# Cross attention: probability transposes and value products taken for two heads at a time

## The chip, the cores and the metric

One core of one Trainium2 chip. The metric is the device time of one execution in microseconds (us), median of repeated runs. All work is fp32: a product is made of three passes of the matrix engine over operands split into a high and a low half (fp32r); transposes and a few small products run in plain fp32.

## The reference, cut to what matters

Two layers, each with two feed-forward blocks, a mixer and a cross attention. The change touches only the cross attention (4 heads of 256 columns, 256 tokens, 256 memory tokens):

```python
hq = (rms_norm(x, xa_norm[l]) @ xa_wq[l]).reshape(b, t, XA_HEADS, XA_HD)
...
s = jnp.einsum("bqhd,bmhd->bhqm", hq, mk).astype(jnp.float32) * (XA_HD ** -0.5)
p = jax.nn.softmax(s, axis=-1).astype(mv.dtype)
o = jnp.einsum("bhqm,bmhd->bqhd", p, mv).reshape(b, t, XA_HEADS * XA_HD)
x = x + o @ xa_wo[l]
```

## The kernel before

Each engine has its own instruction list, written out by hand in the order in which it runs, and the lists meet at semaphores. `xa_pe`, `xa_act` and `xa_dve` each count the events of one engine in the order listed in the code, and `at(l, event)` is the count to wait for. In the cross attention of a layer:

- PE (TensorE) makes the queries of a head with `queries(l, h)` (48 products), its scores with `S(h)` (12 products), transposes its probabilities with `pT(h)` (four fp32 transposes of 128x128), multiplies by the values with `pv(h)` (12 products) and runs the output projection with `o(h)` (48 products, in two halves `n`, of eight column blocks `d` each; `between` is work put ahead of the second half, `midway` ahead of the fifth column block of that half). `last_down` is the projection of head 3. The weight blocks are q4 and q5 (queries of heads 2 and 3) and o0 to o3.
- DVE (VectorE) scales the queries (`hq_scaled`), takes their low half (`hq_lo_part`), finds the row maximum (`row_max`), divides the exponentials by their sum (`normalise`, whose event `p{h}` lets `pT(h)` run), takes the low half of the transposed probabilities (`pT_lo`, whose event lets `pv(h)` run) and of the head's output (`oT_lo`, whose event lets `o(h)` run), and takes the low half of each weight block (`split`).
- ACT (ScalarE) takes the high halves (`hq_hi_part`, `pT_hi`, `oT_hi`, `split`) and the exponentials (`exp`).

`e_sb` and the halves `p_hi`, `p_lo` hold two heads, so heads 0 and 1 go ahead of heads 2 and 3. The PSUM banks are shared: `pT(0)` to `pT(3)` write banks G[2], G[3], G[0], G[1], and scores and value products of head h use G[h].

The weight blocks stream through a ring of three places of 2048 columns. SP loads a block when DVE has split the one that it overwrites, and ACT splits a block (`split_block`) only when PE has multiplied the block whose place it takes:

```python
if BEFORE[i]:
    act.wait_ge(s_blk, BEFORE[i])
```

With the block widths here o1 takes the place of q4, o2 that of q5, and o3 that of o0. So ACT's split of o3 waits until PE has finished `o(0)`. The first two blocks of the second feed-forward block take the place of o1.

Of the kernel before, what the change touches and what calls it, by code (L numbers as in the profile page):

```python
# [20 lines left out]
KD = D // P  # L21
# [177 lines left out]
def hymba_kernel(nc, x_d, mem_d, memT_d, w_d, par_d, const_d, fin_d, out_d):  # L199
    ctx = ExitStack()  # L200
    with ctx:
# [12 lines left out]
        def signals(name, events):  # L214
            return Signals(sem(name), events)
# [166 lines left out]
                                      "sso1 kvlo5 on1 oT0 oT1").split())  # L382
        att_pool = signals("att_pool", ["bias", "ro0", "ro1"])
        xa_pe = signals("xa_pe", "q0 S0 S1 pT0 pT1 pv0 S2 pv1 S3 pT2 pT3 pv2 pv3".split())
        xa_act = signals("xa_act", "hq0 hq1 exp0 exp1 hq2 pT0 hq3 pT1 oT0 oT1 exp2 exp3 pT2 pT3 oT2 oT3".split())
        xa_dve = signals("xa_dve", "hf0 hf1 hq0 hq1 max0 p0 max1 p1 hf2 pT0 hf3 hq2 hq3 pT1 oT0 max2 oT1 p2 max3 p3 pT2 pT3 oT2 oT3".split())

        SCALE = DK ** -0.5
        XSCALE = XD ** -0.5
# [275 lines left out]
        def _(act):  # L665
# [331 lines left out]
            def cross(l):  # L997
                norm_start(4 * l + 2)
                split(l, "q", 4)
                spread_root(4 * l + 2)  # L1000
                A(junk[:, 0:8], eps[:, :], ACT.Exp)
                split(l, "q", 5)

                def hq_hi_part(h):

                    act.wait_ge(xa_dve.sem, xa_dve.at(l, f"hf{h}"))
                    A(hq_hi[:, 2 * h:2 * h + 2, :], HQ_F[h][:, :, :], ACT.Copy).then_inc(xa_act.sem, xa_act.one(f"hq{h}"))

                def exp(h):

                    act.wait_ge(xa_dve.sem, xa_dve.at(l, f"max{h}"))
                    for t in range(TT):
                        last = A(e_sb[:, h % 2, t, :], s_sb[:, t, 0:T], ACT.Exp, bias=nmx[:, 0, 2 * (h % 2) + t:2 * (h % 2) + t + 1],
                                 accum_out=den[:, 2 * (h % 2) + t:2 * (h % 2) + t + 1])
                    last.then_inc(xa_act.sem, xa_act.one(f"exp{h}"))

                def pT_hi(h):

                    act.wait_ge(xa_pe.sem, xa_pe.at(l, f"pT{h}"))
                    A(p_hi[:, 2 * (h % 2):2 * (h % 2) + 2, :], pair(XA_PT[h]), ACT.Copy  # L1020
                      ).then_inc(xa_act.sem, xa_act.one(f"pT{h}"))

                def oT_hi(h):

                    act.wait_ge(xa_pe.sem, xa_pe.at(l, f"pv{h}"))
                    A(a_hi[:, 2 * h:2 * h + 2, :], pair(XA_O[h]), ACT.Copy).then_inc(xa_act.sem, xa_act.one(f"oT{h}"))

                hq_hi_part(0)
                hq_hi_part(1)
                split(l, "o", 0)  # L1030
                exp(0)
                split(l, "o", 1)
                exp(1)
                hq_hi_part(2)
                pT_hi(0)
                hq_hi_part(3)
                pT_hi(1)
                oT_hi(0)
                split(l, "o", 2)
                oT_hi(1)  # L1040
                exp(2)
                exp(3)
                pT_hi(2)
                split(l, "o", 3)
                pT_hi(3)
                oT_hi(2)
                oT_hi(3)
                for i in heads(l, "ffn2"):
                    split_block(i)
# [40 lines left out]
        def _(dve):  # L1090
# [446 lines left out]
            def cross(l):  # L1537
# [60 lines left out]
                    dve.wait_ge(s_mrbc, 1)  # L1598
                row_max(0)
                split(l, "o", 0)  # L1600
                normalise(0)
                row_max(1)
                split(l, "o", 1)
                normalise(1)
                hq_scaled(2)
                pT_lo(0)
                hq_scaled(3)
                hq_lo_part(2)
                hq_lo_part(3)
                pT_lo(1)  # L1610
                oT_lo(0)
                row_max(2)
                oT_lo(1)
                split(l, "o", 2)
                normalise(2)
                row_max(3)
                normalise(3)
                pT_lo(2)
                split(l, "o", 3)
                pT_lo(3)  # L1620
                oT_lo(2)
                oT_lo(3)
                split_block(heads(l, "ffn2")[0])
# [54 lines left out]
        def _(pe):  # L1678
# [135 lines left out]
                        spread_mean_squares(q)  # L1814
                    four_columns(INDEX[l, "in", i], (U, GATE), range(2 * i, 2 * i + 2), ready=8 * q)

            def head_columns(hi, lo, whi, wlo, bank, ks, width, at=0, ready=None, between=None):

                for k in ks:
                    if k == KD // 2 + 1 and between is not None:  # L1820
                        between()
                    if ready is not None:
                        pe.wait_ge(s_alo, ready + k + 1)
                    for d in range(2):
                        out = bank[:, d * T:(d + 1) * T]
                        w = slice((k - ks[0]) * width + at + d * P, (k - ks[0]) * width + at + (d + 1) * P)
                        M(out, whi[:, w], hi[:, k, :], start=(k, d) == (0, 0), stop=False, skip_group_check=True)  # L1827
                        M(out, whi[:, w], lo[:, k, :], start=False, stop=False, skip_group_check=True)  # L1828
                        last = M(out, wlo[:, w], hi[:, k, :], start=False, stop=k == KD - 1, skip_group_check=True)  # L1829
                return last  # L1830
# [28 lines left out]
                            last.then_inc(xa_pe.sem, xa_pe.one("q0"))  # L1859
                    last.then_inc(s_blk, 1)  # L1860

            def queries(l, h, between):

                whi, wlo = weights(INDEX[l, "q", 2 + h])
                head_columns(a_hi, a_lo, whi, wlo, HQ[h], range(KD), T, between=between).then_inc(s_blk, 1)

            def gate_up_blocks(l, f, c):

# [353 lines left out]
            def cross(l):  # L2222
                pe.wait_ge(att_dve.sem, att_dve.at(l, "kvlo5"))
                first_queries(l, 4 * l + 2)

                def S(h):

                    pe.wait_ge(xa_dve.sem, xa_dve.at(l, f"hq{h}"))
                    for t in range(TT):
                        out = XA_S[h][:, t * T:(t + 1) * T]  # L2230
                        for k in range(2 * h, 2 * h + 2):
                            M(out, hq_hi[:, k, tok(t)], kx_hi[:, k, :], start=(t, k) == (0, 2 * h), stop=False)
                            M(out, hq_hi[:, k, tok(t)], kx_lo[:, k, :], start=False, stop=False)
                            last = M(out, hq_lo[:, k, tok(t)], kx_hi[:, k, :], start=False, stop=(t, k) == (1, 2 * h + 1))
                    last.then_inc(xa_pe.sem, xa_pe.one(f"S{h}"))

                def pT(h, tiles=range(TT)):

                    pe.wait_ge(xa_dve.sem, xa_dve.at(l, f"p{h}"))
                    if h >= 2:  # L2240
                        pe.wait_ge(xa_dve.sem, xa_dve.at(l, f"oT{h - 2}"))
                    for t in tiles:
                        for k in range(2):
                            last = TR(XA_PT[h][:, k * T + t * P:k * T + (t + 1) * P],
                                      e_sb[:, h % 2, t, k * P:(k + 1) * P], ident)
                    if tiles[-1] == TT - 1:
                        last.then_inc(xa_pe.sem, xa_pe.one(f"pT{h}"))

                def pv(h):

                    pe.wait_ge(xa_dve.sem, xa_dve.at(l, f"pT{h}"))
                    for d in range(2):
                        out = XA_O[h][:, d * T:(d + 1) * T]
                        w = slice((2 * h + d) * P, (2 * h + d + 1) * P)
                        for k in range(2):
                            p = 2 * (h % 2) + k
                            M(out, vx_hi[:, k, w], p_hi[:, p, :], start=(d, k) == (0, 0), stop=False)
                            M(out, vx_hi[:, k, w], p_lo[:, p, :], start=False, stop=False)
                            last = M(out, vx_lo[:, k, w], p_hi[:, p, :], start=False, stop=(d, k) == (1, 1))
                    last.then_inc(xa_pe.sem, xa_pe.one(f"pv{h}"))  # L2260

                def o(h, between=None, midway=None):

                    pe.wait_ge(xa_dve.sem, xa_dve.at(l, f"oT{h}"))
                    down(l, "o", h, a_hi, a_lo, (2 * h, 2 * h + 1), h == 0, between=between, midway=midway)

                queries(l, 2, between=lambda: S(0))
                S(1)
                queries(l, 3, between=lambda: pT(0))
                pT(1)  # L2270
                pv(0)
                S(2)
                pv(1)
                o(0, between=lambda: S(3), midway=lambda: pT(2, range(1)))
                pT(2, range(1, 2))
                o(1, between=lambda: (pT(3), pv(2)))
                pv(3)
                o(2)
                pe.wait_ge(xa_dve.sem, xa_dve.at(l, "oT3"))
                last_down(4 * l + 2, a_hi, a_lo, (6, 7))  # L2280
# [110 lines left out]
```

## Time and profile before

| | |
|---|---|
| median of 3 runs | 1123.31 us (1123.18 to 1124.47) |
| the profiled execution | 1123.65 us, of which the span of the instructions is 1121.9 us |
| mean granted TensorE clock | 0.999 |
| PE busy | 1112.1 us (99%) |
| DVE, ACT busy | 830.4 us (74%), 628.3 us (56%) |

Matrix instructions are pipelined: a product of 256 columns is shown 0.28 us long, but the next one starts 0.11 us after it. So the pace of PE is read from start to start, and a share of 99% says only that PE seldom had nothing in its pipe.

### The profile page before, as it was taken

Reading aid. Unit: us, or ns where it says so; the run is one execution under the profiler, and the core shown is the slowest. Engines: PE = TensorE matmul, PEld = TensorE weight load, DVE = VectorE, ACT = ScalarE, POOL = GpSimd, SP = SyncE. Lnnn points to the kernel's source line nnn. Section 1 sums busy time; section 2 is a strip of 40 time slices with the busy share of each in tenths; the row PEclk is TensorE's granted clock in tenths of the full one; section 3 lists DMA queues with packets and bytes.
Section 4 is the critical chain, followed back from the end, with each engine's and each line's share of the span. In section 5 each row is a group of like instructions: output and inputs, shape, how many; then the busy total and the mean of one; then the engine's idle time right before and its main releaser. Section 6 shows DMA issues by size and latency. Waiting matters only on the chain.

```text
span 1121.9 us, 20774 instructions
## 1 busy us (share of the span) xinstructions
PE 1112.1 (99%) x8828; PEld 1070.6 (95%) x8828; DVE 830.4 (74%) x1162; ACT 628.3 (56%) x871; POOL 18.0 (2%) x42
## 2 busy tenths in 40 slices
PE   9999999999999999999999999999999999999998
PEld 8999999999899999999999999999999999888886
DVE  7766667999978785655686675589998868866764
ACT  6554555556765654444574554474767756644454
POOL 1000000010000000000000000000100000000000
PEclk9999999999999999999999999999999999999999
DMA  7965654555454376555547655546546444666561
GB/s 269 325 213 188 220 170 175 188 188 185 156 173 164 113 235 223 174 198 193 202 158 247 221 179 194 192 151 208 169 155 221 155 146 150 195 198 209 185 195 52
DMA packets 69932, 211.25 MB, mean 188 GB/s; under 512 B 5072, under 2 KB 28240, under 8 KB 65232
## 3 DMA queue, kind: packets, MB, share of 16 engines
q1 hardware_dynamic: 68864, 209.19, 55.0%
q8 instruction: 70, 1.15, 0.4%
q10 hardware_dynamic: 976, 0.73, 0.2%
q14 instruction: 22, 0.18, 0.0%
HBM read 208.85 MB, written 1.05 MB: 187 GB/s over the span
## 4 chain that ended last, share of the span: by engine, by line
PE 93%; DVE 4%; ACT 1%; DVEq 1%; issue 0%; DMA 0%; ACTq 0%
PE G L1885 10%; PE G L1887 10%; PE G L1886 10%; PE G L1911 8%; PE D L1724 8%; PE D L1716 8%; PE D L1717 8%; PE G L1919 4%; DVE w_lo L1096 2%; PE D L1763 2%; PE D L1761 2%; PE D L1762 2%; PE D L1827 2%; PE D L1829 2%; PE D L1828 2%; PE G L1693 1%
## 5 line engine op out<-in xcount | busy, mean ns | idle before, releaser
L1096 DVE TENSOR_TENSOR w_lo<-w_raw,w_hi 128x2048 fp32r<-128x2048 f32 (+3 forms) x260 | 452.4, 1746 | 106.7 <-ACT w_hi L673 105.6
L673 ACT ACTIVATE w_hi<-w_raw 128x2048 fp32r<-128x2048 f32 (+3 forms) x260 | 383.3, 1481 | 163.6 <-PE G L1887 112.2
L1885 PE MATMUL G<-a,w_hi 128*128 128x256 f32 x990 | 273.7, 276 | 0.3 <-DVE w_lo L1096 0.3
L1887 PE MATMUL G<-a,w_lo 128*128 128x256 f32 x990 | 273.3, 276 | 0.0
L1886 PE MATMUL G<-a,w_hi 128*128 128x256 f32 x990 | 273.3, 276 | 0.0
L1885 PEld LDWEIGHTS G<-a,w_hi 128*128 128x128 f32 x990 | 185.8, 188 | 0.8 <-DVE w_lo L1096 0.5
L1886 PEld LDWEIGHTS G<-a,w_hi 128*128 128x128 f32 x990 | 185.8, 188 | 0.0
L1887 PEld LDWEIGHTS G<-a,w_lo 128*128 128x128 f32 x990 | 185.8, 188 | 0.0
L1717 PE MATMUL D<-hT_lo,w_hi 128*128 128x256 f32 x528 | 145.7, 276 | 0.0
L1716 PE MATMUL D<-hT_hi,w_hi 128*128 128x256 f32 x528 | 145.7, 276 | 0.0
L1724 PE MATMUL D<-hT_hi,w_lo 128*128 128x256 f32 x528 | 145.7, 276 | 0.0
L769 ACT ACTIVATE hT_hi<-zqk 128x256 fp32r<-128x256 f32 x88 | 36.7, 418 | 137.2 <-DVE zqk L1235 137.1
L1911 PE MATMUL G<-a,w_hi 128*128 128x512 f32 x416 | 102.4, 391 | 0.0
L1724 PEld LDWEIGHTS D<-hT_hi,w_lo 128*128 128x128 f32 x528 | 99.1, 188 | 0.0
L1716 PEld LDWEIGHTS D<-hT_hi,w_hi 128*128 128x128 f32 x528 | 99.1, 188 | 0.0
L1717 PEld LDWEIGHTS D<-hT_lo,w_hi 128*128 128x128 f32 x528 | 99.1, 188 | 0.0
L1228 DVE TENSOR_TENSOR zqk<-G,zqk 128x512 f32<-128x512 f32 x62 | 42.7, 689 | 72.8 <-PE G L1887 72.8
L1911 PEld LDWEIGHTS G<-a,w_hi 128*128 128x128 f32 x416 | 75.5, 188 | 13.9
L1716 PE MATMUL D<-a,w_hi 128*128 128x256 f32 x256 | 71.5, 279 | 0.0
L1724 PE MATMUL D<-a,w_lo 128*128 128x256 f32 x256 | 70.8, 277 | 0.0
L1717 PE MATMUL D<-a,w_hi 128*128 128x256 f32 x256 | 70.8, 277 | 0.0
L1919 PEld LDWEIGHTS G<-a,w_lo 128*128 128x128 f32 x416 | 52.1, 188 | 2.7
(309 smaller groups left out, 2085.5 us busy)
## 6 DMA issues: line engine op xcount, KB each, us to landing
w_raw<-w_dram SPq DMA_DIRECT2D x116, 1024.0 KB, 5.0
w_raw<-w_dram SPq DMA_DIRECT2D x151, 512.0 KB, 5.2
m_raw<-memT_dram SPq DMA_DIRECT2D x2, 1024.0 KB, 8.6
w_raw<-w_dram SPq DMA_DIRECT2D x6, 256.0 KB, 5.7
w_raw<-w_dram SPq DMA_DIRECT2D x8, 128.0 KB, 4.4
vx<-mem_dram SPq DMA_DIRECT2D x1, 1024.0 KB, 11.2
out_dram<-vx SPq DMA_DIRECT2D x3, 256.0 KB, 2.2
m_raw<-x_dram SPq DMA_DIRECT2D x2, 256.0 KB, 4.6
```

Source lines behind the costliest of these rows:

```text
L673: A(w_hi[:, part_hi(i)], w_raw[:, part(i)], ACT.Copy).then_inc(s_hi, 1)
L769: A(hT_hi[:, c % SLOTS_H, :], hT[:, :], ACT.Copy).then_inc(s_hhi, 1)
L1096: V.tensor_tensor(w_lo[:, part_lo(i)], w_raw[:, part(i)], w_hi[:, part_hi(i)].bitcast(F32), ALU.subtract).then_inc(s_lo, 1)
L1228: V.tensor_tensor(gu[:, :, :], gu[:, :, :] if twos(l, f, c) else pair(G[gu_bank(l, f, c)]), rinv_bc[:, :].rearrange("p (b t) -> p b t", b= ...
L1716: M(channels(d), whi[:, w], hi[:, k, :], start=start and d % 2 == 0, stop=False, skip_group_check=True)
L1717: M(channels(d), whi[:, w], lo[:, k, :], start=False, stop=False, skip_group_check=True)
L1724: return M(channels(d), wlo[:, w], hi[:, k, :], start=False, stop=stop, skip_group_check=True)
L1885: M(out, whi[:, w], a_hi[:, k, :], start=(k, u) == (0, 0), stop=False, skip_group_check=True)
L1886: M(out, whi[:, w], a_lo[:, k, :], start=False, stop=False, skip_group_check=True)
L1887: last = M(out, wlo[:, w], a_hi[:, k, :], start=False, stop=k == KD - 1, skip_group_check=True)
L1911: last = M(banks[b], whi[k, b], both, start=k == 0 and not low_first, stop=k == KD - 1 and low_first, skip_group_check=low_first)
L1919: last = M(banks[b][:, T:], wlo[k, b], a[:, k, 0, :], start=k == 0 and low_first, stop=k == KD - 1 and not low_first, skip_group_check=low ...
```

## The change

On PE, `pT(0)` and `pT(1)` run together ahead of the seventh of eight steps (`at=6`) of `queries(l, 3)`, instead of one ahead of its sixth step and one behind it. `S(3)` runs ahead of `o(0)` instead of inside it; `pT(2)` and `pT(3)` run together in the middle of the second half of `o(0)`, instead of in three pieces in `o(0)`, behind it and in `o(1)`; `pv(2)` and `pv(3)` run together between the halves of `o(1)`. The lists of ACT and DVE are reordered: ACT takes `hq_hi_part(2)` ahead of `exp(1)`, `pT_hi(1)` ahead of `hq_hi_part(3)`, `exp(2)` ahead of `oT_hi(1)`, and the split of o3 ahead of `pT_hi(2)`. DVE takes `hq_scaled(2)` ahead of `normalise(0)` and moves its splits: o1 from ahead of `normalise(1)` to between `row_max(3)` and `normalise(3)`, o2 from ahead of `normalise(2)` to behind `normalise(3)`, o3 to behind `pT_lo(3)`.

```diff
--- before.py
+++ after.py
@@ -382,8 +382,9 @@
                                       "sso1 kvlo5 on1 oT0 oT1").split())
         att_pool = signals("att_pool", ["bias", "ro0", "ro1"])
         xa_pe = signals("xa_pe", "q0 S0 S1 pT0 pT1 pv0 S2 pv1 S3 pT2 pT3 pv2 pv3".split())
-        xa_act = signals("xa_act", "hq0 hq1 exp0 exp1 hq2 pT0 hq3 pT1 oT0 oT1 exp2 exp3 pT2 pT3 oT2 oT3".split())
-        xa_dve = signals("xa_dve", "hf0 hf1 hq0 hq1 max0 p0 max1 p1 hf2 pT0 hf3 hq2 hq3 pT1 oT0 max2 oT1 p2 max3 p3 pT2 pT3 oT2 oT3".split())
+        xa_act = signals("xa_act", "hq0 hq1 exp0 hq2 exp1 pT0 pT1 hq3 oT0 exp2 oT1 exp3 pT2 pT3 oT2 oT3".split())
+        xa_dve = signals("xa_dve", ("hf0 hf1 hq0 hq1 max0 hf2 p0 max1 hq2 p1 pT0 pT1 hf3 hq3 oT0 max2 oT1 p2 max3 p3 pT2 pT3 oT2 "
+                                    "oT3").split())
 
         SCALE = DK ** -0.5
         XSCALE = XD ** -0.5
@@ -1030,18 +1031,18 @@
                 split(l, "o", 0)
                 exp(0)
                 split(l, "o", 1)
+                hq_hi_part(2)
                 exp(1)
-                hq_hi_part(2)
                 pT_hi(0)
+                pT_hi(1)
                 hq_hi_part(3)
-                pT_hi(1)
                 oT_hi(0)
+                exp(2)
+                oT_hi(1)
                 split(l, "o", 2)
-                oT_hi(1)
-                exp(2)
                 exp(3)
+                split(l, "o", 3)
                 pT_hi(2)
-                split(l, "o", 3)
                 pT_hi(3)
                 oT_hi(2)
                 oT_hi(3)
@@ -1598,26 +1599,26 @@
                     dve.wait_ge(s_mrbc, 1)
                 row_max(0)
                 split(l, "o", 0)
+                hq_scaled(2)
                 normalise(0)
                 row_max(1)
-                split(l, "o", 1)
+                hq_lo_part(2)
                 normalise(1)
-                hq_scaled(2)
                 pT_lo(0)
+                pT_lo(1)
                 hq_scaled(3)
-                hq_lo_part(2)
                 hq_lo_part(3)
-                pT_lo(1)
                 oT_lo(0)
                 row_max(2)
                 oT_lo(1)
-                split(l, "o", 2)
                 normalise(2)
                 row_max(3)
+                split(l, "o", 1)
                 normalise(3)
+                split(l, "o", 2)
                 pT_lo(2)
+                pT_lo(3)
                 split(l, "o", 3)
-                pT_lo(3)
                 oT_lo(2)
                 oT_lo(3)
                 split_block(heads(l, "ffn2")[0])
@@ -1814,10 +1815,10 @@
                         spread_mean_squares(q)
                     four_columns(INDEX[l, "in", i], (U, GATE), range(2 * i, 2 * i + 2), ready=8 * q)
 
-            def head_columns(hi, lo, whi, wlo, bank, ks, width, at=0, ready=None, between=None):
+            def head_columns(hi, lo, whi, wlo, bank, ks, width, at=0, ready=None, between=None, before=None):
 
                 for k in ks:
-                    if k == KD // 2 + 1 and between is not None:
+                    if k == before and between is not None:
                         between()
                     if ready is not None:
                         pe.wait_ge(s_alo, ready + k + 1)
@@ -1859,10 +1860,10 @@
                             last.then_inc(xa_pe.sem, xa_pe.one("q0"))
                     last.then_inc(s_blk, 1)
 
-            def queries(l, h, between):
+            def queries(l, h, between, at=KD // 2 + 1):
 
                 whi, wlo = weights(INDEX[l, "q", 2 + h])
-                head_columns(a_hi, a_lo, whi, wlo, HQ[h], range(KD), T, between=between).then_inc(s_blk, 1)
+                head_columns(a_hi, a_lo, whi, wlo, HQ[h], range(KD), T, between=between, before=at).then_inc(s_blk, 1)
 
             def gate_up_blocks(l, f, c):
 
@@ -2234,17 +2235,16 @@
                             last = M(out, hq_lo[:, k, tok(t)], kx_hi[:, k, :], start=False, stop=(t, k) == (1, 2 * h + 1))
                     last.then_inc(xa_pe.sem, xa_pe.one(f"S{h}"))
 
-                def pT(h, tiles=range(TT)):
+                def pT(h):
 
                     pe.wait_ge(xa_dve.sem, xa_dve.at(l, f"p{h}"))
                     if h >= 2:
                         pe.wait_ge(xa_dve.sem, xa_dve.at(l, f"oT{h - 2}"))
-                    for t in tiles:
+                    for t in range(TT):
                         for k in range(2):
                             last = TR(XA_PT[h][:, k * T + t * P:k * T + (t + 1) * P],
                                       e_sb[:, h % 2, t, k * P:(k + 1) * P], ident)
-                    if tiles[-1] == TT - 1:
-                        last.then_inc(xa_pe.sem, xa_pe.one(f"pT{h}"))
+                    last.then_inc(xa_pe.sem, xa_pe.one(f"pT{h}"))
 
                 def pv(h):
 
@@ -2266,15 +2266,13 @@
 
                 queries(l, 2, between=lambda: S(0))
                 S(1)
-                queries(l, 3, between=lambda: pT(0))
-                pT(1)
+                queries(l, 3, between=lambda: (pT(0), pT(1)), at=6)
                 pv(0)
                 S(2)
                 pv(1)
-                o(0, between=lambda: S(3), midway=lambda: pT(2, range(1)))
-                pT(2, range(1, 2))
-                o(1, between=lambda: (pT(3), pv(2)))
-                pv(3)
+                S(3)
+                o(0, midway=lambda: (pT(2), pT(3)))
+                o(1, between=lambda: (pv(2), pv(3)))
                 o(2)
                 pe.wait_ge(xa_dve.sem, xa_dve.at(l, "oT3"))
                 last_down(4 * l + 2, a_hi, a_lo, (6, 7))
```

## Rows read from the trace of the kernel before

**Rows 1.** The page: chain that ended last, share of the span by engine.

```profile
PE 93%; DVE 4%; ACT 1%; DVEq 1%; issue 0%; DMA 0%; ACTq 0%
```

**Rows 2.** Waits of PE, whole span: us in total, times, longest.

```profile
PE G L2257 <- DVE hT_lo L1582: 2.9, 2, 1.4
```

**Rows 3.** Timeline of PE, layer 0, heads 0 and 1: start, length, line, operands.

```profile
345.99 0.60 PE L2244 MATMUL G<-const,e_sb 128*128 128x128 f32 x4
...
346.67 0.28 PE L1829 MATMUL D<-a,w_lo 128*128 128x256 f32 x1
...
348.49 0.60 PE L2244 MATMUL G<-const,e_sb 128*128 128x128 f32 x4
350.52 0.39 PE L2257 MATMUL G<-hT_hi,vx_hi 128*128 128x256 f32 x1 [1.43 <-DVE hT_lo L1582]
...
354.72 0.28 PE L1716 MATMUL D<-a,w_hi 128*128 128x256 f32 x1
```

**Rows 4.** Timeline of PE, layer 0, heads 2 and 3.

```profile
360.05 0.28 PE L1724 MATMUL D<-a,w_lo 128*128 128x256 f32 x1
...
361.80 0.38 PE L2244 MATMUL G<-const,e_sb 128*128 128x128 f32 x2
...
362.25 0.28 PE L1724 MATMUL D<-a,w_lo 128*128 128x256 f32 x1
...
364.73 0.28 PE L1724 MATMUL D<-a,w_lo 128*128 128x256 f32 x1
...
370.74 0.28 PE L1716 MATMUL D<-a,w_hi 128*128 128x256 f32 x1
```

**Rows 5.** Timeline of DVE, layer 0, cross attention.

```profile
339.88 0.48 DVE L1563 CUSTOM_DVE_ANT_0 gbc<-G,rmem_bc,xs 128x256 f32<-128x256 f32 x1
...
340.85 0.17 DVE L1566 TENSOR_SCALAR nmx<-mx 128x2 f32<-128x2 f32 x1
340.93 2.29 DVE L1096 TENSOR_TENSOR w_lo<-w_raw,w_hi 128x2048 fp32r<-128x2048 f32 x1
343.13 0.16 DVE L1572 RECIPROCAL rden<-den 128x2 f32<-128x2 f32 x1
...
343.90 0.48 DVE L1563 CUSTOM_DVE_ANT_0 gbc<-G,rmem_bc,xs 128x256 f32<-128x256 f32 x1
...
347.91 0.68 DVE L1549 TENSOR_TENSOR accs<-D,std 128x512 f32<-128x512 f32 x1
349.77 0.69 DVE L1582 TENSOR_TENSOR hT_lo<-G,hT_hi 128x512 fp32r<-128x512 f32 x1 [1.18 <-ACT hT_hi L1020]
...
361.42 0.17 DVE L1572 RECIPROCAL rden<-den 128x2 f32<-128x2 f32 x1 [1.16 <-ACT e_sb L1013]
361.67 0.62 DVE L1575 TENSOR_SCALAR e_sb<-e_sb,rden 128x256 f32<-128x256 f32 x2
```

**Rows 6.** Timeline of ACT, layer 0, cross attention.

```profile
341.05 0.51 ACT L1013 ACTIVATE e_sb<-gbc,nmx 128x256 f32<-128x256 f32 x1 [2.19 <-DVE nmx L1566]
...
342.06 1.92 ACT L673 ACTIVATE w_hi<-w_raw 128x2048 fp32r<-128x2048 f32 x1
...
348.62 0.63 ACT L1007 ACTIVATE m<-accs 128x512 fp32r<-128x512 f32 x1 [2.46 <-DVE accs L1549]
349.16 0.58 ACT L1020 ACTIVATE hT_hi<-G 128x512 fp32r<-128x512 f32 x1
...
354.92 0.60 ACT L1026 ACTIVATE a<-G 128x512 fp32r<-128x512 f32 x1 [0.30 <-PE G L2259]
...
360.30 0.51 ACT L1013 ACTIVATE e_sb<-gbc,nmx 128x256 f32<-128x256 f32 x1 [3.80 <-DVE nmx L1566]
...
362.21 0.60 ACT L1020 ACTIVATE hT_hi<-G 128x512 fp32r<-128x512 f32 x1 [0.82 <-PE G L2244]
```

**Rows 7.** Windows: busy time, granted clock (PEclk) of one stretch, layer 0.

```profile
346.00:351.00 5.00, 3.57 (x32) 3.33 (x31) 3.74 (x8) 1.27 (x4) 0.00 (x0) 1.00 0.77 273
```

**Rows 8.** The page: DMA issues of weight blocks, us to landing.

```profile
w_raw<-w_dram SPq DMA_DIRECT2D x151, 512.0 KB, 5.2
```

## The prediction

> **What bounds the kernel now.** I read the chain of work that ended last first: 93% of it is PE [rows 1], so PE's list is the clock of this kernel, and an edit counts only through the time that PE stands still or works slower. Next come PE's own waits: in 1121.9 us the largest is the first product of `pv(0)`, which waits for `pT_lo(0)`, once in each layer, 2.9 us in both [rows 2]. Then the timelines of the three engines through layer 0's cross attention [rows 3 to 6]; the wait has the same length in layer 1, so I work out one layer and double it.
>
> **Prices from the rows.** From the start of `o(0)` at 354.72 to 360.05 PE starts 47 further products: 5.33/47 = 0.1133 us each [rows 3, 4]. A run of four transposes at 345.99 and two products behind it take 0.68 us to the start of the third; a run of two at 361.80 takes 0.45 us [rows 3, 4]. Without the products (0.227) that is 0.453 and 0.225 us: 0.113 a transpose, in proportion, with nothing left for a change between fp32 and fp32r. One effect follows a short run: from 362.25 to 364.73 the 21 products take 0.118 us each [rows 4], 0.0047 more than normal.
>
> **What the change removes.** (1) The wait of `pv(0)`. Transposes from 348.49 are paid by 348.94; `o(0)` starts at 354.72 [rows 3], and 36 products earlier is 350.64. So 1.70 us a layer goes: 1.43 shown idle, the rest an unfilled pipe (0.12 behind the first product at 350.52). (2) Three of five runs: nothing by the proportion, since 16 transposes stay 16. The slow pace of 36 products behind the two runs of two goes, 0.17 us. Together 1.87 us a layer, 3.7 in all. That is the most that this change can give, if PE waits nowhere new.
>
> **What it adds.** I lay the new lists beside each other with the durations of the rows. A DVE instruction is followed by the next about 0.09 us before its shown end (2.29 long, next after 2.20) [rows 5]; so a 512-column operation (0.68) takes 0.60, a `normalise` 0.77 (343.13 to 343.90), a `row_max` 0.97 to its last step and 1.05 to the next instruction (339.88, 340.85, 340.93) [rows 5]. An `exp` starts 0.20 us behind the last step of `row_max` (340.85, 341.05), holds ACT 1.01 (to 342.06) and lets DVE go on 1.12 behind its start (360.30, 361.42) [rows 5, 6]. ACT acts 0.71 behind the start of a DVE operation (347.91, 348.62) and DVE 0.61 behind that of `pT_hi` (349.16, 349.77) [rows 5, 6]. A DVE result at 350.46 (349.77 and 0.69) starts PE at 350.52 [rows 3, 5]. PE's last product starts 0.31 before ACT can take its result (354.61, one product before 354.72, and 354.92); ACT follows a run of transposes 0.41 behind the start of a run of two (361.80, 362.21), so 0.63 behind a run of four [rows 3, 4, 6].
>
> *First pair.* Nothing changes up to DVE's slot at 343.13. Then `hq_scaled(2)` to 343.73, `normalise(0)` to 344.50, `row_max(1)` with its last step at 345.47, `exp(1)` at 345.67, `normalise(1)` at 346.79; its second part starts 0.25 later and is 0.62 long [rows 5], so `p1` is there at 347.66. PE has the sixth step of queries done and begins `pT(0)` at 345.99 + 6 x 0.1133 = 346.67, and would begin `pT(1)` at 347.12, but waits until 347.72: 0.60 us. Whether a run that starts from an empty pipe loses another 0 or 0.13 (as at 350.52) no row shows; I take 0.06, so 0.66. Behind the waiting `pT(1)` stand the last 12 products of the queries, so they hide nothing; they do cover `pT_lo(0)`: `pv(0)` starts at 349.60 without a wait (its operand is there at 348.7). `pv(0)` starts 1.04 us earlier than before.
>
> *Second pair.* `S(2)` ends at 352.32, so `row_max(2)` starts at 352.52 (0.31 behind its last product), `exp(2)` at 353.69, `oT_hi(1)` behind it at 354.70, `oT_lo(1)` 355.33 to 355.93, `normalise(2)` to 356.70, `row_max(3)` to 357.75, then the moved split of o1, 2.20 us, to 359.95, and `normalise(3)`: `p3` is there at 360.82. PE, with 48 products from 349.60, starts `o(0)` at 355.04, `pT(2)` 36 products later at 359.12, and is at `pT(3)` at 359.57. It waits until 360.88: 1.31, and with the same 0.06 1.37 us. Behind it wait the last 12 products of `o(0)`, and for these ACT: its split of o3 overwrites o0 and needs all of `o(0)`, and now stands ahead of `pT_hi(2)`.
>
> *Value products of the second pair.* `o(0)` ends at 359.57 + 1.37 + 0.453 + 1.36 = 362.76. The split of o3 starts at 362.96 and holds ACT 1.83 us (1.92 less the overlap) [rows 6], `pT_hi(2)` starts at 364.79, `pT_lo(2)` at 365.41, 0.69 long, and PE may go at 366.16, with the unfilled pipe 366.28. PE comes to `pv(2)` 24 products behind `o(0)`, at 365.48. Wait 0.80 us.
>
> *Moved at no cost.* The split of o1 ends near 360 instead of 347, so SP's load of the first feed-forward blocks starts that much later; it lands in about 5.2 us [rows 8], at 365, and PE and ACT ask for that place only after `o(1)`, beyond 371. With a load twice as long that cover would be gone. The splits of o2 and o3 end near 363 and 369, ahead of `o(2)` and `last_down`.
>
> **The sum.** Added 0.66 + 1.37 + 0.80 = 2.83, removed 1.87, so 0.96 us a layer later: `o(2)` starts at 371.70 instead of 370.74 [rows 4]. Two layers: +1.9 us. The profiled execution takes 1123.65 (span 1121.9), so 1125.55; it lies 0.34 above the median, 1123.31, so the median after should be 1125.2. Bounds: no loss at the restarted transposes, 0.24 less in all, 0.13 at each, 0.28 more.
>
> **Rivals.** *The slow pace stays* (slower by more). A run of eight may leave the 0.118 pace that the runs of two left [rows 4], against it the runs of four [rows 3] leave none. It would stretch the 36 products up to the end of `S(2)` by 0.17 us a layer (what follows is swallowed by the waits); with the full 0.13 at both restarts, +2.5 in all: 1125.8.
>
> *One new wait is not there.* If DVE is past `normalise(3)` about 1.3 us earlier than I add up, `pT(3)` doesn't wait; each of its links is a row, but the order of two engines must mesh as I laid it. Then 0.4 us a layer less than before: 1122.5.
>
> *The runs themselves cost* (faster). If each switch into and out of fp32 costs more than the proportion shows, six fewer switches pay. To reach the faster side it has to cover the new waits and 2.25 us more, 4.2 / 6 = 0.7 us a run. With 0.75: 1120.7. Runs of two and four in proportion [rows 3, 4] speak against it.
>
> *The clock.* PE gets 1.00 of its clock, the 2.4 GHz level, in the stretch from 346 to 351, in which the two runs of four transposes and the 1.43 us wait lie [rows 7]. In the new order the longest stretch without a product is `pT(2)`, wait and `pT(3)`, 0.45 + 1.37 + 0.45 = 2.3 us, against 0.45 + 1.70 = 2.15 before. If that dropped the clock to 1.2 GHz for the 36 products up to `pv(2)`, at twice the pace, 4.1 us come on top, of which the wait at `pv(2)` takes up 0.8: +6.6 in two layers, 1131.8. The Trainium skill, "TensorE: Matmul & The Clock Gate", Part 4: PE-mode transpose, says that transposes don't count as PE activity for the clock gate, which would make longer runs of them a risk; by that rule the sum would be this one, and the trace, with 1.00 over nearly as long a stretch, gives it little room.
>
> **How the numbers follow.** No change here means within 0.2%, 2.25 us: about what a measurement of this kernel can tell. Forecast (two of the three waits at least as priced): 0.67, from 1124.3 to 1126.0; the upper quarter of it lies above 1125.56. Slow pace: 0.15, two thirds above. One wait missing: 0.11. Runs cost: 0.05. Clock: 0.02. So slower 0.17 + 0.10 + 0.02 = 0.29, faster 0.05, same 0.66. The range takes in the case with one wait missing and the slow pace with half a microsecond of the runs' own scatter (1123.18 to 1124.47): 1122.2 to 1126.4.
>
> **What would show it.** Right: PE waits in each layer at the second run of the first pair, about 0.6 us for `normalise(1)`, at the second run of the second pair, about 1.3 us for `normalise(3)`, and at `pv(2)`, about 0.7 us for `pT_lo(2)` with ACT's split of o3 right before `pT_hi(2)`; no wait at `pv(0)`; `o(2)` some 1 us later behind the start of the layer's first queries. Wrong: runs of eight that take clearly more or less than 0.91 us without a wait, `p3` ahead of PE, a granted clock under 1.00, or a wait at `o(0)`, `o(2)` or in the feed-forward block behind.

## The result and the profile after

The median after is 1126.14 us (1125.18 to 1127.58, 21 runs), beside 1124.03 us before (1123.18 to 1124.78, 21 runs). The ratio is 1.0019, with an interval from 1.0013 to 1.0025: 2.1 us more, just inside what counts as no change here (0.2%), though the interval reaches beyond it. The profiled execution takes 1125.55 us, the sum that the prediction makes for it; its span is 1123.7 us, 1.8 more than before. That the two agree to the hundredth is chance: 14 of the 21 executions take longer, up to 1127.58 us.

The chain by engine on the page of after still belongs to PE, with one per cent less than in [rows 1]:

```profile
PE 92%; DVE 5%; ACT 2%; DVEq 1%; issue 0%; ACTq 0%
```

Waits of PE of after, whole span (us in total, times, longest):

```profile
PE G L2245 <- DVE e_sb L1576: 2.6, 4, 0.8
...
PE G L2257 <- DVE hT_lo L1583: 1.0, 2, 0.5
```

The 2.9 us of [rows 2] are gone and 3.6 us stand in their place, on other instructions: four runs of transposes wait for `normalise`, and two value products, now those of `pv(2)`, wait for `pT_lo(2)`.

Timeline of PE of after, layer 0 (start, length, operands, idle time and releaser):

```profile
346.40 0.60 PE L2245 MATMUL G<-const,e_sb 128*128 128x128 f32 x4
347.44 0.66 PE L2245 MATMUL G<-const,e_sb 128*128 128x128 f32 x4 [0.45 <-DVE e_sb L1576]
347.86 0.36 PE L1828 MATMUL D<-a,w_hi 128*128 128x256 f32 x1
...
349.35 0.28 PE L2257 MATMUL G<-hT_hi,vx_hi 128*128 128x256 f32 x1
...
359.25 0.60 PE L2245 MATMUL G<-const,e_sb 128*128 128x128 f32 x4
360.69 0.66 PE L2245 MATMUL G<-const,e_sb 128*128 128x128 f32 x4 [0.84 <-DVE e_sb L1576]
...
365.94 0.39 PE L2257 MATMUL G<-hT_hi,vx_hi 128*128 128x256 f32 x1 [0.50 <-DVE hT_lo L1583]
...
371.50 0.28 PE L1717 MATMUL D<-a,w_hi 128*128 128x256 f32 x1
```

Against [rows 3] and [rows 4] the reader is to see four things. `pv(0)` at 349.35 has no wait. The second run of each pair and `pv(2)` have one. `o(2)` starts at 371.50. And from 349.35 to 359.25 the 84 products (`pv(0)`, `S(2)`, `pv(1)`, `S(3)` and 36 of `o(0)`) take 9.90 us, 0.1179 each instead of 0.1133 (called the slow pace below). All of layer 0 stands 0.27 us earlier than before (the frame, below), since a wait of PE of 0.2 us at the start of the program is missing in this execution.

What holds them back, first in the timeline of DVE of after:

```profile
357.58 2.28 DVE L1097 TENSOR_TENSOR w_lo<-w_raw,w_hi 128x2048 fp32r<-128x2048 f32 x1
359.79 0.16 DVE L1573 RECIPROCAL rden<-den 128x2 f32<-128x2 f32 x1
360.02 0.62 DVE L1576 TENSOR_SCALAR e_sb<-e_sb,rden 128x256 f32<-128x256 f32 x2
...
365.20 1.29 DVE L1583 TENSOR_TENSOR hT_lo<-G,hT_hi 128x512 fp32r<-128x512 f32 x2 [2.36 <-ACT hT_hi L1021]
```

And in the timeline of ACT of after:

```profile
362.76 1.93 ACT L674 ACTIVATE w_hi<-w_raw 128x2048 fp32r<-128x2048 f32 x1 [3.96 <-PE D L1725]
364.59 1.06 ACT L1021 ACTIVATE hT_hi<-G 128x512 fp32r<-128x512 f32 x2
```

The moved split of o1 ends right ahead of `normalise(3)`, for whose `p3`, there at 360.64, PE is waiting. ACT's split of o3 waits for the last product of `o(0)` and then holds up `pT_hi(2)` and `pT_hi(3)` for 1.83 us.

Windows of after (busy time of PE with its instructions in brackets first, PEclk third from the right):

```profile
346.40:349.35 2.95, 2.50 (x22) 2.27 (x21) 2.06 (x5) 1.29 (x4) 0.00 (x0) 1.00 0.24 94
349.35:359.25 9.90, 9.90 (x86) 9.90 (x85) 7.14 (x19) 5.72 (x12) 0.00 (x0) 1.00 0.00 0
359.25:361.40 2.15, 1.31 (x12) 1.07 (x11) 2.07 (x5) 0.00 (x0) 0.00 (x0) 1.00 0.14 32
```

As in [rows 7], PE keeps the 2.4 GHz level through both pairs of runs, and through the slow products between them.

### The profile page after: what moved, and what is told of

Same layout as the page of the kernel before. It is cut to its first block, busy times and chain, and to the rows that moved or that the text cites. A ratio compares the mean times of both kernels' runs of the same rounds, so it can differ in the third digit from the quotient of the medians.

```text
span 1123.7 us, 20772 instructions
## 1 busy us (share of the span) xinstructions
PE 1113.4 (99%) x8828; PEld 1071.3 (95%) x8828; DVE 831.1 (74%) x1162; ACT 628.5 (56%) x871; POOL 18.0 (2%) x42
## 3 DMA queue, kind: packets, MB, share of 16 engines
HBM read 208.85 MB, written 1.05 MB: 187 GB/s over the span
## 4 chain that ended last, share of the span: by engine, by line
PE 92%; DVE 5%; ACT 2%; DVEq 1%; issue 0%; ACTq 0%
PE G L1886 10%; PE G L1887 10%; PE G L1888 10%; PE G L1912 8%; PE D L1718 7%; PE D L1717 7%; PE D L1725 7%; PE G L1920 4%; DVE w_lo L1097 2%; PE D L1764 2%; PE D L1763 2%; PE D L1762 2%; PE D L1828 2%; PE D L1830 2%; PE D L1829 2%; PE G L1694 1%
```

## The experiments

To compare the kernels by place and not only by total, I use one stretch per layer: from the layer's first run of fp32 transposes (in the mixer, line 2129 of after, 262.62) to the first product of 512 columns in the second feed-forward block (393.49). Each is read from one profiled execution, start to start; the ratio is that of the times of all executions. What differs between two executions outside the two stretches, up to 0.9 us here, is no part of the first two columns.

| kernel | layer 0, us | layer 1, us | ratio to before, interval |
|---|---|---|---|
| before | 129.84 | 118.56 | |
| after | 130.87 | 119.59 | 1.0019 [1.0013, 1.0025] |
| o3 behind pT_hi | 129.95 | 118.67 | 0.9996 [0.9987, 1.0005] |
| o1 behind normalise | 129.81 | 118.54 | 0.9994 [0.9985, 1.0003] |
| pT(1) behind queries | 131.18 | 119.92 | 1.0022 [1.0012, 1.0032] |
| PE's order alone | 132.60 | 121.47 | 1.0049 [1.0035, 1.0064] |
| split of o2 ahead too | 135.59 | 121.82 | 1.0081 [1.0067, 1.0096] |
| four runs, no waits | 129.42 | 117.71 | 0.9976 [0.9967, 0.9985] |
| the same again | 129.43 | 117.71 | 0.9983 [0.9974, 0.9992] |
| runs ahead of the projection | 129.50 | 117.79 | 0.9991 [0.9982, 1.0000] |
| runs of one | 129.59 | 117.87 | 0.9989 [0.9980, 0.9998] |
| small wait in four runs | 128.70 | 117.99 | 0.9978 [0.9969, 0.9987] |

After loses 1.03 us in each layer: the whole loss lies in this stretch. The two waits at the second pair of heads are tested by the first two experiments, one each; the wait at the first pair by the third.

**The split of o3 behind pT_hi.** Against after, on ACT:

```diff
                 exp(3)
-                split(l, "o", 3)
                 pT_hi(2)
                 pT_hi(3)
+                split(l, "o", 3)
```

> The changed kernel stands 2.1 us behind the kernel before. Theory (three new waits, one after the other): with ACT's split of o3 behind pT_hi(2) and pT_hi(3), pT_lo(2) is there at about 363.4 us in layer 0, ahead of PE's arrival at pv(2) (365.28), so the wait of pv(2) (0.50 us idle, 0.77 us with the unfilled pipe) is gone and nothing else moves: 1.5 us less in two layers, +0.6 us against the kernel before. Rival (the longer fp32 runs and the slower pace behind them are what costs): PE's list is untouched, so no change, +2.1 us.

Measured: 0.9996, no difference from before; 0.92 us a layer less than after. Waits of PE in this kernel, cross attention:

```profile
PE G L2245 <- DVE e_sb L1576: 3.1, 4, 1.1
```

The wait at `pv(2)` is gone, so ACT's split made it. The other wait has grown from 0.84 to 1.12 us: behind the first pair the products ran at 0.1133 us here, although PE's list is that of after, and PE came earlier to a `p3` that did not. A window of that stretch of this kernel, with 89 instructions of PE in 9.80 us, where after has 86 in 9.90 (the last three are already transposes of `pT(2)`; the 84 products alone take 9.53 us, from 349.46 to 358.99):

```profile
349.50:359.30 9.80, 9.80 (x89) 9.80 (x88) 7.13 (x19) 5.72 (x12) 0.00 (x0) 1.00 0.00 0
```

More was won (0.92) than the wait had cost (0.78), the rest by the pace.

**The split of o1 behind normalise(3).** Against after, on DVE:

```diff
                 row_max(3)
-                split(l, "o", 1)
                 normalise(3)
+                split(l, "o", 1)
                 split(l, "o", 2)
```

> DVE's split of o1 behind normalise(3) instead of ahead of it. Theory: p3 comes at about 359.7 us in layer 0 instead of 360.64, pT(3) waits about 0.1 us instead of 0.99, o(1) now waits about 0.3 us for the split of o1, and the wait of pv(2) shrinks from 0.77 to about 0.6: some 0.8 us less a layer, +0.4 us against the kernel before. Rival (runs and pace): no change, +2.1 us.

Measured: 0.9994; 1.05 us a layer less than after, like before. Waits of PE:

```profile
PE G L2245 <- DVE e_sb L1576: 1.2, 4, 0.4
...
PE D L1717 <- DVE w_lo L1097: 0.5, 2, 0.2
```

The wait for `p3` falls to 0.17 us in layer 0, and a smaller one appears: `o(1)` waits for the low half of its own block, which is now split later. So the split of o1 ahead of `normalise(3)` made the larger wait, and its move behind it pays even with the new wait. The wait at `pv(2)` is as good as gone too (0.02 us in layer 0), since `o(0)`, for which ACT's split of o3 waits, ends earlier. The products behind the first pair go at 0.1133 us in this kernel also; that gives little here, as PE still comes to `pT(3)` ahead of `p3`.

**pT(1) behind the queries.** Against after, on PE:

```diff
-                queries(l, 3, between=lambda: (pT(0), pT(1)), at=6)
+                queries(l, 3, between=lambda: pT(0), at=6)
+                pT(1)
```

> pT(1) behind queries(l, 3) instead of in it: three runs a layer, and 12 products lie over the wait for p1. Theory: the wait of pT(1) (0.64 us) is gone, but pT_lo(1), hq_hi_part(3) and oT_lo(0) come later on DVE, row_max(2) starts 0.25 us later, and PE gives the gain back at pT(3), which waits about 1.9 us instead of 0.99: 0.25 us more a layer, +2.6 us against the kernel before. Rival (each run costs): one run more in each layer, also slower, but with a wait of pT(3) that does not grow. Rival (each wait counts by itself): 1.3 us less, +0.8 us.

Measured: 1.0022, not less than after. Waits of PE:

```profile
PE G L2245 <- DVE e_sb L1576: 3.7, 2, 1.8
...
PE G L2257 <- DVE hT_lo L1583: 1.0, 2, 0.5
```

Two waits of the four are gone and the other two are 1.85 us long instead of 0.84: `p3` comes when DVE has it, and PE, sooner past the first pair, only stands longer at the second. So the wait at the first pair is not the last on its path, and gives nothing when it is taken away. Four of the eleven executions of this kernel had a lower mean granted clock, which the section on the hardware takes up.

**PE's order alone.** Against before, only those parts of the change's diff that concern PE:

```diff
-                queries(l, 3, between=lambda: pT(0))
-                pT(1)
+                queries(l, 3, between=lambda: (pT(0), pT(1)), at=6)
...
+                S(3)
+                o(0, midway=lambda: (pT(2), pT(3)))
+                o(1, between=lambda: (pv(2), pv(3)))
```

> One part of the change alone: PE's new list, with the lists of ACT and DVE as they were before. Theory (the waits follow from the three lists together): p1 comes behind the split of o1 and PE waits 0.95 us for it, pT_lo(0) comes behind hq_scaled(2) and pv(0) waits 0.7 us, p3 waits for exp(2) behind the split of o2 (1.7 us), pv(3) waits 1.1 us for pT_lo(3) behind the split of o3: about 1.6 us a layer more than in the changed kernel, +5.4 us against the kernel before (the changed kernel: +2.1). Rival (two runs instead of five are a gain that reordering ACT and DVE spoils): faster than the changed kernel, below +2.1 us.

Measured: 1.0049, 5.5 us. Waits of PE:

```profile
PE G L2244 <- DVE e_sb L1575: 4.5, 4, 1.6
PE G L2256 <- DVE hT_lo L1582: 2.6, 4, 0.9
```

Eight waits, 7.1 us in all, against 2.9 before. PE's new order by itself costs 5.67 us in the two stretches; the reordering of ACT and DVE, which comes with it in after, gives back 3.61 of that.

**The split of o2 ahead of normalise(3) too** (a larger dose of the same wait). Against after, on DVE:

```diff
                 split(l, "o", 1)
-                normalise(3)
                 split(l, "o", 2)
+                normalise(3)
```

> The changed kernel with DVE's split of o2, 2.20 us, also ahead of normalise(3): a second dose of the same cost. Theory: p3 comes 2.2 us later, PE waits about 3.2 us at pT(3) instead of 0.99, nothing gives it back: 2.2 us more a layer, +6.5 us against the kernel before. Rival (the wait of pT(3) is covered by other work): less than half of that, under +4.3 us.

Measured: 1.0081, 9.1 us. The waits at the second pair are 3.32 and 3.05 us, as expected from one more split, and all waits of the cross attention 8.1 us (7.3 and 0.8) instead of 3.6 in after. With the 2.06 us of after that makes 6.6; 2.4 more in the two stretches are not waits. Windows of this kernel around the second pair, layer 0 and then layer 1, up to and behind the end of the wait (PE busy is the second value, PEclk the third from the right), then PE's timeline around `pv(2)` in layer 0:

```profile
358.50:362.40 3.90, 0.64 (x6) 0.41 (x5) 3.82 (x5) 0.00 (x0) 0.00 (x0) 1.00 0.43 119
362.40:366.00 3.60, 3.54 (x17) 3.54 (x18) 0.00 (x1) 0.00 (x0) 0.00 (x0) 0.53 0.93 310
...
917.20:920.80 3.60, 0.60 (x6) 0.36 (x4) 3.52 (x5) 0.00 (x0) 0.00 (x0) 1.00 0.45 129
920.80:924.40 3.60, 3.55 (x30) 3.55 (x31) 0.00 (x0) 1.44 (x1) 0.00 (x0) 1.00 0.97 344
...
368.22 0.28 PE L1725 MATMUL D<-a,w_lo 128*128 128x256 f32 x1
...
368.56 0.28 PE L1725 MATMUL D<-a,w_lo 128*128 128x256 f32 x1
369.29 0.39 PE L2257 MATMUL G<-hT_hi,vx_hi 128*128 128x256 f32 x1 [0.45 <-DVE hT_lo L1583]
...
369.63 0.28 PE L2259 MATMUL G<-hT_hi,vx_lo 128*128 128x256 f32 x1
...
369.99 0.28 PE L2259 MATMUL G<-hT_hi,vx_lo 128*128 128x256 f32 x1
```

In layer 0 PE, once its transposes may go, gets about half of its clock, the 1.2 GHz level, until 366: 17 instructions in 3.6 us where layer 1, behind a wait only 0.27 us shorter, has 30. So the prediction's clock rival is a real mechanism of this chip and this place, but not of the change: there the wait is 0.84 us long, and the mean granted clock of all 21 executions is 0.998 to 1.000. The 2.4 us are found: by my estimate the lower clock cost 1.6 us (four transposes and 13 products take 3.59 us, from 362.46 to 366.05, instead of 1.99), and the slow pace 0.8 net over both layers, against after. In layer 0 it is missing behind the first pair and begins only behind the short wait at `pv(2)`: three products take 0.34 us ahead of that wait and 0.36 behind it, with no transpose between.

**Four runs, placed where nothing waits.** Against after, PE takes its four runs of four apart, and each list sets the operand ahead of the splits:

```diff
-                queries(l, 3, between=lambda: (pT(0), pT(1)), at=6)
+                queries(l, 3, between=lambda: pT(0), at=6)
+                pT(1)
...
-                o(0, midway=lambda: (pT(2), pT(3)))
-                o(1, between=lambda: (pv(2), pv(3)))
+                o(0, midway=lambda: pT(2))
+                o(1, between=lambda: (pT(3), pv(2)))
+                pv(3)
```

On ACT the split of o3 stands between `pT_hi(2)` and `pT_hi(3)`; on DVE the split of o1 stands behind `row_max(2)` and that of o2 between `pT_lo(2)` and `pT_lo(3)`.

> Four runs of four transposes a layer, placed so that products lie over every chain: pT(1) behind the queries, pT(2) in o(0), pT(3) ahead of pv(2) in o(1), pv(3) behind o(1); ACT takes pT_hi(2) ahead of the split of o3; DVE splits o1 where it idles behind row_max(2) and takes pT_lo(2) ahead of the split of o2. Theory (only waits cost, runs cost nothing): no wait of PE over 0.1 us in the cross attention, o(2) starts about 2.5 to 2.9 us earlier a layer than in the changed kernel: -2.9 to -3.7 us against the kernel before. Rival (runs cost): four runs instead of two, slower than the changed kernel by the cost of four switches, or at least less of a gain than the waits removed.

Measured: 0.9976, and 0.9983 when it ran again; PE waits nowhere in the cross attention. It beats both kernels, the one before by about 0.2%. It gives 0.42 and 0.85 us in the two layers instead of the 1.7 of the removed wait, and the trace shows why. PE in this kernel, layer 0:

```profile
366.54 0.28 PE L1717 MATMUL D<-a,w_hi 128*128 128x256 f32 x1
...
366.90 0.28 PE L1717 MATMUL D<-a,w_hi 128*128 128x256 f32 x1
...
367.25 0.28 PE L2257 MATMUL G<-hT_hi,vx_hi 128*128 128x256 f32 x1
```

Three products take 0.35 to 0.36 us: the pace of 0.118, behind `pT(1)` from 348.04 to 357.9 and behind `pT(3)` from 362.93 to 391.4, where products of 512 columns begin. Over the 84 and some 240 products at 0.0045 us this is 1.5 us in layer 0; in layer 1, with 84 and 144, it is 1.0.

**The runs ahead of projection products, and runs of one.** First, the kernel of four runs with `pT(0)` moved ahead of the sixth step of the queries, `pT(1)` ahead of the last, and `pT(3)` into the first half of `o(1)`, so that projection products follow each run instead of value products:

```diff
-                queries(l, 3, between=lambda: pT(0), at=6)
-                pT(1)
+                queries(l, 3, between=lambda k: pT(0 if k == 5 else 1), at=(5, 7))
...
-                o(1, between=lambda: (pT(3), pv(2)))
+                o(1, early=lambda: pT(3), between=lambda: pv(2))
```

Second, the same with the transposes of heads 2 and 3 one at a time between projection products, 12 more runs in the program:

```diff
-                o(0, midway=lambda: pT(2))
-                o(1, early=lambda: pT(3), between=lambda: pv(2))
+                o(0, each=(1, lambda i: pT_one(2, i)))
+                o(1, between=lambda: pv(2), each=(0, lambda i: pT_one(3, i)))
```

> Four runs of four as in e4, but each is followed by products of the queries or of the projection instead of by value products: pT(0) and pT(1) ahead of the sixth and the eighth step of queries(l, 3), pT(2) in the second half of o(0), pT(3) in the first half of o(1). In e4 the pace was 0.118 us behind pT(1) (84 products) and behind pT(3) (some 240 products, up to the 512-column products of the feed-forward block). Theory (a run of four directly ahead of value products leaves the slow pace, one ahead of projection products does not): 1.4 us less a layer than e4, no waits: about -5.5 us against the kernel before. Rival (the pace is a chance of the build): as e4, -2.4 to -2.7 us, with the slow pace behind some of the runs.

> As e7, but each of the eight transposes of heads 2 and 3 stands alone between the products of the projection: eight runs of one instead of two of four. Theory (a transpose costs 0.11 us wherever it stands, switches cost nothing): the stretch from the first of them to o(2) is as long as in e7 up to 0.1 us, if the pace behind them stays at 0.1133; a pace of 0.118, as behind the runs of two, would add 0.2 us a layer up to o(2), and up to 1.1 us a layer if it lasts into the feed-forward block. Rival (a switch costs): six more runs a layer, 12 in all, at the 0.09 us that the first product behind a run comes late, +1.1 us or more already inside o(0) and o(1).

Measured for the first: 0.9991, against an expected gain of 5.5 us. The slow pace stands behind `pT(1)` and `pT(3)` as before, so that theory falls: what follows a run does not set the pace. Measured for the second: 0.9989, 0.09 and 0.08 us longer than the first in the two layers. Twelve more changes into fp32 and back cost 0.17 us, 0.014 each; the rival that runs themselves cost something needed 0.7.

**A small wait in the four runs, and the four runs again.** The kernel of four runs with `pv(3)` drawn ahead of the second half of `o(1)`, where it just meets `pT_lo(3)`:

```diff
-                o(1, between=lambda: (pT(3), pv(2)))
-                pv(3)
+                o(1, between=lambda: (pT(3), pv(2), pv(3)))
```

> Against four_runs_no_waits this moves value product 3 up, to directly behind value product 2 and ahead of the second half of output projection 1, so that it meets the lower half of the probabilities of head 3 (finished at 364.45 to 364.52 us in that run's trace, when PE would be there at 364.42): a wait of 0.1 to 0.2 us, once per layer, and 0.1 us of restart. Theory (an empty PE ends the slow pace of 0.118 us per product): the products behind the wait come every 0.1133 us instead of 0.1178 us; about 216 products in layer 0 and 120 in layer 1 lie behind it, so -1.0 and -0.5 us, less the waits of 0.2 to 0.3 us each: -0.8 and -0.2 us, 1.0 us below the kernel of four runs, -3.3 us against the kernel before. Rival (the pace is set by something else, such as the instructions themselves): the pace stays 0.118 us and the waits are added, +0.4 to +0.6 us above the kernel of four runs, -2.0 us against the kernel before.

> The kernel of four_runs_no_waits once more, on the same chip as the kernel with the small wait: the stand for it. If the slow pace belongs to the program, its two stretches per layer (behind the transposes of head 1 and behind those of head 3) are where they were, and the time is again 2.4 to 2.7 us below the kernel before. If the slow pace falls by chance on each execution, its stretches lie elsewhere or are missing.

Measured: 1121.56 and 1122.18 us, the intervals overlapping widely. In the trace layer 0 is 0.73 us shorter than in the four runs (expected 0.8), layer 1 is 0.28 longer (expected 0.2 shorter). Timeline of PE with the small wait, layer 0 and then layer 1:

```profile
364.67 0.28 PE L2259 MATMUL G<-hT_hi,vx_lo 128*128 128x256 f32 x1
364.95 0.39 PE L2257 MATMUL G<-hT_hi,vx_hi 128*128 128x256 f32 x1
...
365.76 0.28 PE L2257 MATMUL G<-hT_hi,vx_hi 128*128 128x256 f32 x1
...
366.10 0.28 PE L2257 MATMUL G<-hT_hi,vx_hi 128*128 128x256 f32 x1
...
916.04 0.28 PE L2259 MATMUL G<-hT_hi,vx_lo 128*128 128x256 f32 x1
916.33 0.39 PE L2257 MATMUL G<-hT_hi,vx_hi 128*128 128x256 f32 x1
...
916.80 0.28 PE L2257 MATMUL G<-hT_hi,vx_hi 128*128 128x256 f32 x1
...
917.15 0.28 PE L2257 MATMUL G<-hT_hi,vx_hi 128*128 128x256 f32 x1
```

The same wait, about 0.16 us late and an empty pipe, comes in both layers; in layer 0 three products take 0.34 us from 365.76 on, in layer 1 they go on taking 0.35 up to the products of 512 columns. So an empty pipe does not by itself end the slow pace. The kernel of four runs showed its slow stretches in the same places when it ran again, on another chip: as far as two executions tell, the pace is no chance of one execution. Yet PE's list alone does not set it, since the two layers of one execution, with the same list, differ here. What sets it stays open.

## Why the prediction was right

- **PE's list is the clock.** The totals above follow PE's stretches to within some 1.5 us; the intervals of most reach 1 us to either side. The loss of 1.03 us a layer, twice, less the 0.27 us of the earlier frame, is the 1.8 us of the span.
- **The removed wait** is removed: `pv(0)` starts behind the queries without one.
- **First pair: 0.60 and 0.06 forecast.** PE would have begun the second run at 346.40 + 0.45 = 346.85 and began at 347.44: 0.59. The restart: two products and the run take 0.73 us to the next product at 348.17, 0.05 above the normal 0.68.
- **Second pair: 1.31 forecast, 0.99 measured** (360.69 against 359.70). Here the step "starts `o(0)` at 355.04, `pT(2)` 36 products later" was mis-sized: at the slow pace the 84 products take 0.39 us longer, so PE came later to a `p3` that came almost when it should (360.64, forecast 360.82 less the frame of 0.27). The rival of the slow pace thus came true as well as the forecast. Its price was nearly swallowed, as it said of what follows: 0.39 lost ahead of the wait and 0.32 of it returned by the wait. That leaves 0.07, where the rival had 0.17. So the sum came out near because the slow pace and the shorter wait nearly cancel; the forecast's own sum has neither.
- **`pv(2)`: 0.80 forecast.** From 360.69, with the run, 36 products and 0.06, PE would be there at 365.28; 365.94 and 0.12 for the unfilled pipe make 0.78. The first two experiments confirm the causes one at a time: ACT's split of o3 for this wait, DVE's split of o1 for the one at `p3`.
- **The sum: 0.96 a layer forecast, 1.03 measured.** `o(2)` starts at 371.50, against 370.74 [rows 4] less 0.27. The forecast median, 1125.2, was counted from 1123.31, the median of three runs; 21 runs of the same kernel give 1124.03, so 0.72 of the 0.94 us by which 1126.14 lies above the forecast comes from there and not from the change.
- **Runs cost next to nothing**, as the proportion of [rows 3, 4] said: 0.014 us each by the runs of one. So the stated purpose, two runs instead of five, had nothing to win; all that could be won was the wait.
- **The clock** held at 1.00. The Trainium skill, "TensorE: Matmul & The Clock Gate", Part 4: PE-mode transpose, by which transposes don't count as PE-busy the same way, would have made the stretches at the second pair a risk; here 2.15 us with eight transposes and a wait kept 1.00, and the traces show a fall only behind the 3.32 us wait of the larger dose. No run here tells whether the transposes counted for anything in it.

## What to carry to other kernels

When work is grouped on the busiest engine, the first thing to price is the operand of the group's last member: it must now be ready as early as the first one's, and whatever large independent operation stands ahead of it on its own engine (here a 2.2 us split) becomes a wait. Lay the lists of all engines beside each other with measured durations; of several new waits on one path, only what the last one does not swallow counts, so taking an early one away can give nothing. The better order here came from placing and not from grouping: four runs of four, each where its operand is just ready, with the splits behind what PE waits for. Cutting them into runs of one won nothing further.

## What the hardware showed that was not expected

Products of 256 columns go at 0.1133 or at 0.118 us for long stretches, 84 to 240 products, mostly behind runs of fp32 transposes, with a granted clock of 1.00 in either case. With one list of PE the slow pace followed the first pair in after and not in the two kernels that differ from it only in the place of one split on ACT or DVE some 10 us later; in the larger dose, the same list again, it followed the first pair in layer 1 alone. A run of transposes is not needed for it: in layer 0 of the larger dose it began behind the short wait at `pv(2)`. Where it lasted as long, it ended in layer 0 at products of 512 columns; in layer 1 of after the groups of eight products between those of 512 columns have it too, from 936.85 on, although the 144 ahead of them go at 0.1133. Waits do not end it reliably: once, in layer 0 only, it ended some six products behind a short one; in layer 1 of the larger dose it went on behind a wait of 3.05 us (30 PE instructions in the 3.6 us). It is worth up to 1.5 us a layer, nearly as much as the 1.70 us of the removed wait, and its cause is not found.

In the one trace that shows it, the granted clock fell to the 1.2 GHz level behind a wait of 3.32 us between two runs of transposes (0.53 over 3.6 us), and not behind one of 3.05 us in the other layer. The clocks of the executions without a trace suggest that shorter waits can do it as well. With `pT(1)` behind the queries, where the waits at the second pair are 1.85 us, four of eleven executions have a mean granted clock of 0.996 or 0.997 and take 1127.36 to 1130.65 us; the other seven, the profiled one among them, have 0.999 or 1.000 and take 1125.75 to 1126.55. In the larger dose all five have 0.995 to 0.997. Where in these executions the clock fell was not traced.
